# A Griffin and mixture-of-experts layer: tokens' high and low parts in one product of 512 columns for the sixteen transposed blocks, with another opening order

## The reference

```
xn = rms_norm(x);  z = xn @ w_in           # 1024 -> 7168 columns
rnn_x, rnn_gate, q, k, v, g_rnn, g_attn = split(z)
xc = causal_depthwise_conv(rnn_x)          # 4 taps over tokens
hr = rg_lru(xc)                            # gates, exp, scan over tokens
y_rnn = (hr * gelu(rnn_gate)) @ w_proj_rnn
y_attn = attention(rotary(q), rotary(k), v) @ w_proj_attn    # 8 heads, causal
x = x + (sigmoid(g_rnn) * y_rnn + sigmoid(g_attn) * y_attn) @ w_out
x = x + moe(rms_norm(x))                   # top 4 of 32 experts, SwiGLU
return rms_norm(x)
```

## Time and profile before

| | us |
|---|---|
| median of 3 runs (lowest, highest) | 1171.51 (1171.34, 1171.87) |
| the profiled execution | 1172.5 |
| its span, first to last instruction | 1170.8 |
| TensorE matmul busy | 1104.9 (94%) |
| VectorE busy | 361.3 (31%) |
| ScalarE busy | 236.7 (20%) |
| mean DMA rate | 384 GB/s |
| the chain that ended last | PE 56%, DMA 37%, DVE 4%, ACT 2% |

### The profile page before, as it was taken

The page is one execution under the profiler, slowest core; times in us unless marked ns, Lnnn a source line. Parts: engine busy times, 40 slices in busy tenths (PEclk is TensorE's granted clock), DMA queues, the critical chain, the costliest instruction groups (busy, mean ns, idle before and its releaser), DMA issues.

```text
span 1170.8 us, 17324 instructions
## 1 busy us (share of the span) xinstructions
PE 1104.9 (94%) x7579; PEld 559.4 (48%) x7579; DVE 361.3 (31%) x677; ACT 236.7 (20%) x435; POOL 7.9 (1%) x22
## 2 busy tenths in 40 slices
PE   8999999999999999999998989898989889898997
PEld 8999888884333333333333333333333333333332
DVE  7747975555121112211111111111111111111112
ACT  6678566343000000000000000000000000000002
POOL 0000000001000000000000000000000000000000
PEclk9999999999999999999999999999999999999999
DMA  9655557699999999999999999999999999999995
GB/s 275 256 188 181 198 216 269 242 405 399 428 427 432 429 430 429 429 433 429 432 431 430 434 433 433 430 431 432 432 430 431 434 432 431 433 431 431 430 424 224
DMA packets 46125, 449.17 MB, mean 384 GB/s; under 512 B 6145, under 2 KB 9281, under 8 KB 29890
## 3 DMA queue, kind: packets, MB, share of 16 engines
q1 hardware_dynamic: 45664, 447.70, 91.8%
q10 hardware_dynamic: 418, 0.84, 0.4%
HBM read 446.96 MB, written 1.05 MB: 383 GB/s over the span
## 4 chain that ended last, share of the span: by engine, by line
PE 56%; DMA 37%; DVE 4%; ACT 2%; issue 1%; SPq 0%; ACTq 0%; DVEq 0%
DMA dn_whole<-in_w_down 34%; PE ps L910 14%; PE ps L851 12%; PE ps L900 6%; PE ps L566 6%; PE ps L572 3%; PE ps L828 2%; PE ps L545 2%; PE ps L549 2%; PE ps L546 2%; DMA dn<-in_w_down 2%; PE ps L756 1%; PE ps L779 1%; PE ps L819 1%; DMA land<-in_w_in 1%
## 5 line engine op out<-in xcount | busy, mean ns | idle before, releaser
L851 PE MATMUL ps<-gu,xg 128*64 128x512 f32 x1920 | 418.7, 594 | 1.3 <-DMA gu<-in_w_gu 1.3
L851 PEld LDWEIGHTS ps<-gu,xg 128*64 128x64 f32 x1920 | 135.0, 137 | 271.7 <-issue 264.0
L910 PE MATMUL ps<-dn_whole,actT 128*64 128x512 f32 x672 | 161.9, 638 | 33.4 <-DMA dn_whole<-in_w_down 33.4
L1757 DVE TENSOR_SCALAR g<-ps 128x512 f32<-128x512 f32 x32 | 22.1, 692 | 441.2 <-PE ps L851 433.8
L910 PEld LDWEIGHTS ps<-dn_whole,actT 128*64 128x64 f32 x672 | 49.6, 146 | 144.6 <-issue 95.2
L1332 ACT ACTIVATE act_s<-g 128x512 f32<-128x512 f32 x25 | 15.7, 630 | 443.0 <-DVE g L1757 443.0
L1715 DVE TENSOR_TENSOR xg<-ps,vec 128x512 f32<-128x512 f32 x31 | 21.4, 690 | 178.9 <-PE ps L779 178.9
L1307 ACT ACTIVATE y_hi<-ps,stat 128x512 fp32r<-128x512 f32 x31 | 21.3, 687 | 250.2 <-PE ps L910 168.1
L900 PE MATMUL ps<-dn,actT 128*64 128x512 f32 x320 | 70.9, 594 | 0.6 <-DMA dn<-in_w_down 0.4
L545 PE MATMUL ps<-x_hi,w_hi 128*128 128x256 f32 x256 | 64.3, 288 | 1.1 <-DVE x_lo L1425 1.1
L546 PE MATMUL ps<-x_lo,w_hi 128*128 128x256 f32 x256 | 63.1, 283 | 0.0
(11 more groups left out here) (269 smaller groups left out, 1019.1 us busy)
## 6 DMA issues: line engine op xcount, KB each, us to landing
gu<-in_w_gu SPq DMA_DIRECT2D x52, 4096.0 KB, 30.8
dn_whole<-in_w_down SPq DMA_DIRECT2D x21, 4096.0 KB, 20.7
dn<-in_w_down SPq DMA_DIRECT2D x20, 2048.0 KB, 13.9
gu<-in_w_gu SPq DMA_DIRECT2D x18, 2048.0 KB, 13.4
land<-in_w_in SPq DMA_DIRECT2D x13, 2048.0 KB, 8.0
gu<-in_w_gu SPq DMA_DIRECT2D x12, 1024.0 KB, 8.4
land<-in_w_proj_rnn SPq DMA_DIRECT2D x2, 2048.0 KB, 7.8
land<-in_w_proj_attn SPq DMA_DIRECT2D x2, 2048.0 KB, 8.9
```

The lines of the kernel that those rows point to most:

```text
L851: last = mm(ps[64 * h:64 * h + 64, 4 + c, :], xg[:, k * SLOTS:(k + 1) * SLOTS], gu[par][m // 2][:, m % 2 * 2 + r, c * D + h * HALF:c * D + ...
L910: last = mm(ps[64 * h:64 * h + 64, bank, :], actT[:, j // 2, j % 2 * SLOTS:(j % 2 + 1) * SLOTS], dn_whole[:, j, h * HALF:(h + 1) * HALF], ...
```

## The change

`x_hi` and `x_lo` lie side by side in one tile `x_both`. For each high weight tile one product of 512 columns writes hi x hi into the first and hi x lo into the second half of a whole PSUM bank; the low weights' products with `x_hi` (256 columns) are added to the second half. A block takes two banks, and two pairs of banks alternate. ScalarE copies the first halves out as before (`evict`), and VectorE adds the second halves to that copy: `add_rest(h)`, at the end of `split_both(h + 2)`. A new semaphore `summed` counts these adds; TensorE's block h waits for `summed` h-1, as do the convolutions, the swaps, gelu and block 16. In blocks 2 and on the order of a piece stays; in blocks 0 and 1 the second piece's high products come before the first piece's low ones. Convolutions move: 0 and 1 behind blocks 2 and 3, 2 and 3 behind 4, 4 and 5 behind 5 and 6, 6 and 7 behind 7 and 8.

In the opening, VectorE sums the squares of the second half of the tokens; `xs` is made in four parts of 2x256 columns; transposes go in the order of tiles i, i+4 into bank 4+i; `x_lo` follows `x_hi` tile by tile, `split_lo(0)` comes after all `x_lo`; 33 warm-up transposes instead of 36. The counts on `evicted` lose their lead of 4.

```diff
--- before
+++ after
@@ -39,7 +39,7 @@
-WARM = 36
+WARM = 33
@@ -110,7 +110,8 @@
-        x_hi, x_lo = at("x_hi", 112, [P, KT, T], f32r), at("x_lo", 168, [P, KT, T], f32r)
+        x_both = at("x_both", 112, [P, 2, KT, T], f32r)
+        x_hi, x_lo = x_both[:, 0], x_both[:, 1]
@@ -214,6 +215,7 @@
+        summed = sem("summed")
@@ -225,6 +227,7 @@
+        ss1_ready = sem("ss1_ready")
@@ -527,27 +530,39 @@
             for t in range(TT):
-                pe.wait_ge(xs_ready, t + 1)
-                for k in range(KT):
-                    last = nc.tensor.transpose(ps[:, 4 + k // 2, (k % 2) * T + t * P:(k % 2) * T + (t + 1) * P],
-                                               xs[:, t, k * P:(k + 1) * P], ident[:, :])
-                    if t == TT - 1 and k % 2 == 1:
+                for i in range(4):
+                    if i % 2 == 0:
+                        pe.wait_ge(xs_ready, 2 * t + i // 2 + 1)
+                    for k in (i, i + 4):
+                        last = nc.tensor.transpose(ps[:, 4 + i, k // 4 * T + t * P:k // 4 * T + (t + 1) * P],
+                                                   xs[:, t, k * P:(k + 1) * P], ident[:, :])
+                    if t == TT - 1:
                         last.then_inc(xT_filled, 1)
-            def transposed(h, bank, src_hi, src_lo, base=0, first=False):
-
-                for c in range(2):
-                    b = (2 * h + c) % PIECES
-                    to = ps[:, bank, c * T:(c + 1) * T]
-                    pe.wait_ge(hi_ready, base + (2 * h + c + 1))
+            def both_at_once(h):
+
+                def times_hi(c):
+                    pe.wait_ge(hi_ready, 2 * h + c + 1)
                     for k in range(KT):
-                        if first and c == 0:
+                        if h == 0 and c == 0:
                             pe.wait_ge(xT_ready, k + 1)
-                        mm(to, w_hi[:, b, k, :], src_hi[:, k, :], start=k == 0, stop=False)
-                        mm(to, w_hi[:, b, k, :], src_lo[:, k, :], start=False, stop=False)
-                    pe.wait_ge(lo_ready, base + (2 * h + c + 1))
+                        mm(ps[:, h % 2 * 2 + c, :], w_hi[:, (2 * h + c) % PIECES, k, :], x_both[:, :, k, :],
+                           start=k == 0, stop=False)
+
+                def times_lo(c):
+                    pe.wait_ge(lo_ready, 2 * h + c + 1)
                     for k in range(KT):
-                        last = mm(to, w_lo[:, b, k, :], src_hi[:, k, :], start=False, stop=k == KT - 1)
-                last.then_inc(filled, 1)
+                        last = mm(ps[:, h % 2 * 2 + c, T:2 * T], w_lo[:, (2 * h + c) % PIECES, k, :], x_hi[:, k, :],
+                                  start=False, stop=k == KT - 1)
+                    return last
+
+                times_hi(0)
+                if h < 2:
+                    times_hi(1)
+                    times_lo(0)
+                else:
+                    times_lo(0)
+                    times_hi(1)
+                times_lo(1).then_inc(filled, 1)
@@ -617,8 +632,9 @@
             for h in range(16):
-                pe.wait_ge(evicted, h + 1)
-                transposed(h, h % 4, x_hi, x_lo, first=h == 0)
+                if h >= 2:
+                    pe.wait_ge(summed, h - 1)
+                both_at_once(h)
                 if 5 <= h < 9:
@@ -644,7 +660,7 @@
                 if i == 0:
-                    pe.wait_ge(evicted, 4 + 20)
+                    pe.wait_ge(evicted, 20)
                 if i >= 1:
@@ -659,12 +675,12 @@
-                    pe.wait_ge(evicted, h + 2)
+                    pe.wait_ge(summed, h // 2 + 7)
...
-                    pe.wait_ge(evicted, h + 2)
+                    pe.wait_ge(evicted, h - 2)
@@ -1097,15 +1113,13 @@
-            for _ in range(4):
-                act.nop().then_inc(evicted, 1)
...
+            act.wait_ge(x_landed[0], 16)
+            A(xc[:, 0:4, :], x_sb[:, 0, :].rearrange("p (c t) -> p c t", c=4), ACT.Square,
+              accum_out=ss[:, 0:1]).then_inc(ss_ready, 1)
...
-                act.wait_ge(x_landed[t], 16)
-                A(xc[:, 4 * t:4 * t + 4, :], x_sb[:, t, :].rearrange("p (c t) -> p c t", c=4), ACT.Square,
-                  accum_out=ss[:, t:t + 1]).then_inc(ss_ready, 1)
-                act.wait_ge(ss_ready, t + 1)
+                act.wait_ge((ss_ready, ss1_ready)[t], 1)
@@ -1124,8 +1138,8 @@
                     z = (z_x, z_gate, z_q, z_k)[h // 4]
-                    A(z[:, 2 * (h % 4):2 * (h % 4) + 2, :], ps[:, h % 4, :].rearrange("p (c t) -> p c t", c=2),
-                      ACT.Copy).then_inc(evicted, 1)
+                    b = h % 2 * 2
+                    A(z[:, 2 * (h % 4):2 * (h % 4) + 2, :], ps[:, b:b + 2, 0:T], ACT.Copy).then_inc(evicted, 1)
                 elif h % 2 == 1:
@@ -1145,9 +1159,11 @@
-                if k % 2 == 0:
-                    act.wait_ge(xT_filled, k // 2 + 1)
-                A(x_hi[:, k, :], ps[:, 4 + k // 2, (k % 2) * T:(k % 2 + 1) * T], ACT.Copy,
+                if k < 4:
+                    act.wait_ge(xT_filled, k + 1)
+                else:
+                    act.wait_ge(xT_ready, k - 3)
+                A(x_hi[:, k, :], ps[:, 4 + k % 4, k // 4 * T:(k // 4 + 1) * T], ACT.Copy,
@@ -1165,7 +1181,7 @@
-                act.wait_ge(evicted, 4 + 12 + 4 * i)
+                act.wait_ge(summed, 12 + 4 * i)
@@ -1200,7 +1216,7 @@
-            act.wait_ge(evicted, 4 + 8)
+            act.wait_ge(summed, 8)
@@ -1237,7 +1253,7 @@
-            act.wait_ge(evicted, 4 + 28)
+            act.wait_ge(evicted, 28)
             A(z_gr[:, :, :], z_gr[:, :, :], ACT.Sigmoid).then_inc(zsig_ready, 1)
@@ -1403,11 +1419,19 @@
             V.memset(spare, 1.0).then_inc(spare_ready, 1)
+            dve.wait_ge(x_landed[1], 16)
+            V.scalar_tensor_tensor(out=xc[:, 4:8, :].rearrange("p c t -> p (c t)"), in0=x_sb[:, 1, :], scalar=1.0,
+                                   in1=x_sb[:, 1, :], op0=ALU.mult, op1=ALU.mult,
+                                   accum_out=ss[:, 1:2]).then_inc(ss1_ready, 1)
             for t in range(TT):
...
                 dve.wait_ge(var_ready, t + 1)
-                V.tensor_scalar(xs[:, t, :], x_sb[:, t, :], rstd[:, t:t + 1], None, ALU.mult).then_inc(xs_ready, 1)
+                to, of = (z[:, t, :].rearrange("p (h c) -> p h c", h=2) for z in (xs, x_sb))
+                for h in range(2):
+                    columns = slice(256 * h, 256 * h + 256)
+                    V.tensor_scalar(to[:, :, columns], of[:, :, columns], rstd[:, t:t + 1], None,
+                                    ALU.mult).then_inc(xs_ready, 1)
             dve.wait_ge(vec_landed, 16)
@@ -1418,15 +1442,13 @@
-            split_lo(0)
             for k in range(KT):
-                if k % 2 == 0:
-                    dve.wait_ge(xT_hi, k + 2)
-                V.scalar_tensor_tensor(out=x_lo[:, k, :], in0=ps[:, 4 + k // 2, (k % 2) * T:(k % 2 + 1) * T],
+                dve.wait_ge(xT_hi, k + 1)
+                V.scalar_tensor_tensor(out=x_lo[:, k, :], in0=ps[:, 4 + k % 4, k // 4 * T:(k // 4 + 1) * T],
                                        scalar=vec[:, V_GMIX, k:k + 1], in1=x_hi[:, k, :].bitcast(f32),
...
-            for q in range(1, PIECES):
+            for q in range(PIECES):
                 split_lo(q)
@@ -1443,10 +1465,10 @@
             def conv(j):
-                if j % 2 == 0:
-                    dve.wait_ge(evicted, 4 + j // 2 + 1)
-                    if j == 0:
-                        dve.wait_ge(ss_ready, TT)
+                if j == 0:
+                    dve.wait_ge(ss_ready, 1)
+                    dve.wait_ge(ss1_ready, 1)
+                dve.wait_ge(summed, j // 2 + 1)
                 z = z_x[:, j, :]
@@ -1459,10 +1481,19 @@
+            def add_rest(h):
+
+                dve.wait_ge(evicted, h + 1)
+                z = (z_x, z_gate, z_q, z_k)[h // 4][:, 2 * (h % 4):2 * (h % 4) + 2, :]
+                b = h % 2 * 2
+                V.tensor_tensor(z, z, ps[:, b:b + 2, T:2 * T], ALU.add).then_inc(summed, 1)
+
             def split_both(h):
...
                 split_lo(2 * h + 1)
+                if h < 18:
+                    add_rest(h - 2)
@@ -1485,12 +1516,10 @@
-            for h in range(2, 6):
-                split_lo(2 * h)
-                conv(2 * (h - 2))
-                split_lo(2 * h + 1)
-                conv(2 * (h - 2) + 1)
-            split_both(6)
+            for h, js in enumerate(((0,), (1,), (2, 3), (4,), (5,)), start=2):
+                split_both(h)
+                for j in js:
+                    conv(j)
             V.memset(gates[:, :, :], 0.0)
@@ -1498,6 +1527,8 @@
                 split_both(h)
+                if h < 9:
+                    conv(h - 1)
             gate_input(0)
...
             split_both(12)
```

## The result

The changed kernel takes 1183.16 us in the median of 4 runs (1182.20 to 1184.78), the one before 1171.42: ratio 1.010, 95% interval 1.0087 to 1.0113. It is slower, as forecast, but by 11.7 us instead of 5.7, and outside the range. The profiled execution took 1182.20 us, span 1180.5.

A forecast was written before the change was run, and what follows sets the result against it. Up to 126 us TensorE's products and one VectorE string bound it, nearly level. Late 2.9 at block 5, minus 1.5, plus 1.55 at the q swap, 4 x 0.62 and 0.3: 5.7 on 1171.5, 1177.2 us; range 1171.5 to 1180.0.

The forecast's parts named there:

- The products: TensorE's sixteen blocks: two 256-column products become one of 512, 0.216 us less a block, 3.4 us saved in all.
- Rival C: TensorE's blocks: the strided 512-column product is no faster than two of 256; 1.5 us not won back, 1178.7; chance 0.14.
- the estimate of 0.6: TensorE's products by the skill's rule of N / 2.4 + 2.5 ns each: the whole merge worth 0.6 us.
- The new wait: TensorE's block h waits for `add_rest(h-2)` behind VectorE's low splits: 2.9 us late at block 5, 1.4 at block 12.
- rival B: The third weight block lands earlier, at 31 us; block 5 starts at 41.7, 2.1 earlier: 1175.1; chance 0.14.
- The q swap: `swap_rope(0)` on ScalarE waits for `add_rest(11)`; its DMA issue moves from 89.03 to 91.98, 2.95 us late.
- The string: VectorE's work from 94.31 us to `scores`, now with four adds: 4 x 0.62 plus 0.3 us of waits, `scores` at 131.8.
- After 126 us: From 126 us on: the same instructions, shifted; nothing changes but the counts waited for, the 5.7 us stay.
- rival D: Between 126 and 260 us: slack of TensorE, VectorE and DMA takes the delay in, 1171.5 to 1173.5; chance 0.08.
- Rival A: String of 94 to 126 us: VectorE's adds find room, TensorE stays the bound, 3.4 us saved, 1168.1; chance 0.12.

The follow-up runs named there:

- the filled wait: Changed kernel, weight blocks 8 and 10 waiting for the q and k swaps, TensorE's wait ahead of block 16 filled with ten products: 1176.38 us (1.0034).
- small adds: Changed kernel, weight blocks 8 and 10 waiting for the q and k swaps, adds of 128x8 instead of 128x512: 1174.16 us (1.0011).
- the adds and copies first: Changed kernel, blocks 8 and 10 waiting for the swaps, all adds ahead of the low splits, ScalarE's copies ahead also in turns 8 to 15: 1169.71 us (0.9979).
- the k swap first: Changed kernel, SyncE issues weight block 10 only when the k swap's two DMAs have landed: 1178.94 us (1.0061).
- both first: Changed kernel, weight block 10 waits for the k swap's landing and block 8 for the q swap's: 1178.02 us (1.0053).
- the early adds first: Changed kernel, blocks 8 and 10 waiting for the swaps, adds ahead of the low splits up to block 9: 1175.02 us (1.0030).
- all adds first and the old copies: Changed kernel, loads waiting for the swaps, all adds ahead of the low splits, ScalarE's copies from turn 8 on still behind its splits: 1174.67 us (1.0024).

## Why the prediction was wrong

*The products* did speed up, by a little less than forecast: 512-column ones of the new operand stand 0.230 us apart in the changed kernel (the chain has eight from 81.26 us on in 1.84) against 0.2265 assumed, which those of the blocks by rows still take at full clock (eight in 1.81), and two of 256 took 0.240. The merge is worth some 2.6 us of TensorE's time, not 3.4. Rival C falls, and with it the estimate of 0.6.

*The new wait* was right as a mechanism, in its places and mostly in size. TensorE waited for adds at blocks 2, 5, 14, 15 and 16: 1.02, 0.78, 1.31, 0.87, 2.73 us, forecast 1.3, 1.1, 1.5, 0.85, 3.1. At block 4 the forecast was 1.4 us: ScalarE's split of the third weight block was taken to stand until 32.99 as before, but it began at 31.64, block 4 at 35.74, with no wait worth a mark. That is rival B in part, and it accounts for block 12 at 86.69 instead of 87.63. The executions scatter by more than the two kernels differ: in the twelve profiled executions this split starts between 30.97 and 33.46 us, and in the two runs with the adds behind the splits where it came late (33.46 with the filled wait, 32.88 with small adds) TensorE did wait at block 4, 1.78 and 1.29 us. So block 4's wait was right as a mechanism too, and the kernel before, read from one trace, was too thin a source for its time.

*The q swap* was right in its issue: 91.03, forecast 91.98. That it then took over twice as long, behind another 2 MB block, was missed; VectorE waited 0.27 us for it, so it cost next to nothing there.

*The string* is the step that failed, in its sentence that the wait for `rot_k` grows from 0.96 to 2.0 us "since the swap stands behind two splits and an add more". The term that was wrong is the swap's time from issue to landing, taken from the trace of before as 4.04 us, and it measured 9.2; the wait was 7.14 us. I had moved the swap past the split that releases SyncE's next block, and had checked that the block had time enough, not what it would do to the swap. Turning this order round gives back 4.2 to 5.1 us; the forecast was 6.0 short (1183.16 less 1177.2). At `scores` the account closes: 5.2 us more for the swap, less 0.6 as its issue came earlier, and 0.6 for the slow products of the next paragraph are the 5.2 by which `scores` missed the forecast in the chain (136.97 against 131.8).

*Slow products behind a wait* stood nowhere in the sum. In the changed kernel the granted clock is 0.50 from 132 to 134 us, behind the wait of 2.78 us, and the sixteen products between 131.74 and `scores` take 5.23 us (2.07, 2.25 and 0.91 in the chain) instead of 3.63 (0.91, 1.81, 0.91). VectorE's last rotation ends at 136.33, so without the slow ones `scores` would have come an estimated 0.6 us earlier and no more. Those behind the wait of block 16 cost nothing there, since TensorE waits again at block 18.

*After 126 us* was right: 10.9 us at `scores` are 10.4 at the last expert, 9.7 in the profiled span and 11.7 in the medians. The forecast's rival D falls.

Rival A, that VectorE's adds find room, was not what the change does, but what it could do: with the adds and copies first they do find room: `scores` 2.7 us earlier, 2.5 us in the time (0.0021 of the 1172.29 beside it), which is about what the merge is worth. What the forecast said against A, that the string would end late in any case, held only for the order given.

## What to carry to other kernels

When a change moves an instruction that issues a DMA, look for every other issue that it passes on the way, and for the semaphore that releases that one: a small transfer on the critical path that falls behind a 2 MB one takes over twice as long (7.3 to 7.8 us against 3.3 here). When an accumulation is split between two engines, put the second engine's part at the head of its queue, as soon as its input is there, and the release of the buffer with it; placed behind the next block's work it ties the first engine's pace to all of that. And allow, above a wait of TensorE of some 3 us, for slow products behind it: here they cost up to 1.6 us in some executions and nothing in others. And read a landing time from more than one trace before a forecast of 1 or 2 us rests on it.

## What the runs showed of the hardware

A 128 KB transfer within on-chip memory took 3.3 to 3.4 us with no load issued just ahead of it, and 7.3 to 7.8 us (medians of two) beside a 2 MB load issued 0.5 to 0.6 us before the first of them, in three kernels. A 2 MB load issued behind the swap, 1 us after the first of its two transfers, didn't slow it: 3.3 us in the kernel before. TensorE's granted clock fell to 1.2 GHz after the wait of 2.7 us ahead of block 16 in some executions and not, or hardly, in others: with the k swap first the first eight products behind that wait took 2.12 us, with both first 2.86, with the early adds first 3.68, with all adds first and the old copies 2.11. ScalarE's split of the third weight block, which waits for its load, started at 31.64 us in the changed kernel and at 32.99 in the one before, and between 30.97 and 33.46 over the twelve profiled executions; the two with both swaps first and with the filled wait are the same program up to block 16 and had it at 31.16 and 33.46. Why it varies is not known.
